# Levels 1 to 4 of a triangular inverse kept as 32 columns per chunk instead of 64

## The chip, the cores and the metric

The kernel runs on one core of one Trainium2 chip. The metric is the device time of one execution in microseconds (us). It was run three times: 2844.94, 2845.5 and 2848.97, median 2845.5. Besides these, one execution was profiled.

## What is computed

A block of two stacked layers on 256 tokens of width 2048. Nearly all of the time goes to its large products with streamed weights. In between stands a recurrent scan (16 heads of 64, two directions, over a context of 256 tokens and then over the 256 tokens of x):

```python
def wkv_scan(r, w, k, v, kk, a, s0, reverse):
    def step(s, inp):
        r_t, w_t, k_t, v_t, kk_t, a_t = inp
        sa = jnp.einsum('bhij,bhj->bhi', s, -kk_t)
        s = (s * w_t[:, :, None, :] + sa[..., None] * (kk_t * a_t)[:, :, None, :]
             + v_t[..., None] * k_t[:, :, None, :])
        return s, jnp.einsum('bhij,bhj->bhi', s, r_t)
    ...
    s_fin, ys = lax.scan(step, s0, xs, reverse=reverse)
```

The kernel computes it in chunks of 64 tokens. Within a chunk the recurrence becomes a linear system, whose 64x64 matrix is triangular with ones on the diagonal, and its inverse is wanted.

## The kernel before

**Units.** The scan is the stretch from about 455 to 880 us of the span. It runs 16 units, `unit(b, q)`: b counts 8 pairs of heads, q is 0 for the context and 1 for x. A unit holds two directions (`d` = 0 and 1), two heads (partitions 0 to 63 and 64 to 127, `HEADS`) and 4 chunks (`NC`) in the free dimension. So a tile of one direction is 128 partitions x 4 x 64 fp32 columns.

**The inverse.** It is built by doubling, levels 0 to 5, with diagonal blocks of 1, 2, 4, ... 32 that become 2, 4, ... 64 wide. POOL masks the matrix for the levels 0 to 4 (`mask_levels`, L990, tiles `lev`, the step named `m0` to `m4`). Level 0 is work of DVE alone: X = I - lev0 (L2058, step X0) and its transpose XT (L2060, step T0). A level `l` from 1 to 4 is then this chain, for each direction:

1. PE, step `Y{l}`: 8 products of lev (the weights, 64x64) with XT (64 moving columns), one for each chunk and head
2. ACT, step `Yb{l}`: copies the result out of PSUM (L1337)
3. PE, step `T{l}`: 8 products of X (the weights) with that copy (64 moving columns)
4. DVE, step `T{l}`: XT = XT - result (L2073)
5. DVE, step `X{l}`: a transpose of XT in blocks of 32x32 gives X (L2043). A level's matrices are zero outside the two diagonal 32x32 blocks, so that this suffices

Y of the next level needs only step 4; step 5 is needed by the PE's T of the next level. Level 5 joins the two 32x32 blocks with 32x32 products (`last_level`, L2690 and L2698, and DVE L2069). XY is a tile with two halves: index 0 holds X, index 1 the copy of step 2.

**Order.** Each engine has its own instruction list, written out by hand, and executes it in order; semaphores (`Steps`, names of steps per direction and q) hold it where it must wait. Both directions alternate in each list. Behind T, PE has other work of the unit as filler (`between`: 12 of 16 records of MV products at levels 1 and 2, a turn of a pair at levels 3 and 4, and in a unit with q = 0 also L2765 and L2743 at level 4). DVE and ACT carry the preparation of the next unit behind each level (`front`, `key`, `group_norm`).

A matmul in fp32 appears as two records in the trace. So one step of both directions, 16 products, shows as 32 records; `each` (L2679) issues them, alternating between the two heads, that is, between two 64x64 quarters of the array.

Of the kernel before, what the change touches and what calls it, by code (L numbers as in the profile page):

```python
# [222 lines left out]
def constants():  # L223
# [24 lines left out]
    for d in range(2):  # L248
# [4 lines left out]
        while size < C:  # L253
# [5 lines left out]
                           np.stack([-(np.arange(P) // SUB % 2 == d).astype(f) for d in range(2)], 1)], 1).astype(f)  # L259
# [22 lines left out]
def program(nc, A, out):  # L282
# [143 lines left out]
    kscan = at("kscan", R + 40 * KIB, [P, 2 * SCAN_DIR + NC * PITCH + C + P + 2])  # L426
# [6 lines left out]
    minus_rows = kscan[:, 2 * SCAN_DIR + NC * PITCH + C + P:]  # L433
# [47 lines left out]
    sub_cols = lambda k: slice(k * SUB, (k + 1) * SUB)  # L481
# [425 lines left out]
    with nc.Block() as block:  # L907
# [162 lines left out]
        def _(act):  # L1070
# [240 lines left out]
            def unit(b, q, ahead=True, norm=None):  # L1311
# [289 lines left out]
        def _(dve):  # L1601
# [429 lines left out]
            def unit(b, q, ahead=True, norm=None):  # L2031
# [438 lines left out]
        def _(pe):  # L2470
# [621 lines left out]
```

How the kernel before makes its waits and increments, by code:

```python
    def wait(self, eng, name, rounds=0):  # L177
        eng.wait_ge(self.sem, self.value(name, rounds))
# [13 lines left out]
    def wait(self, value):  # L192
        self.eng.wait_ge(self.sem, value)
# [607 lines left out]
    def side_step(eng, side):  # L801
        lane, seq, k = side.lane, side.seq, side.k
        tile, c = side_tile(side)
        acc = accs[lane][side.group][:, :]
        if len(tile.shape) == 3:
            acc = acc.rearrange("p (k n) -> p k n", n=CN)
        if seq == 0:
            eng.wait_ge(x_spilled, 16)
            eng.wait_ge(csil_ready, 2)
            eng.wait_ge(mod_used, MOD_CHUNKS)
            eng.wait_ge(mcol_ready, MODS)
        if k == 0 and side.group == 2:
            eng.wait_ge(mcol_ready, MODS + 1)
        eng.wait_ge(raw_in[c.buffer], c.load * 16)
        weight = gain[:, 3, k:k + 1]
        if k == 0:
            ins = eng.tensor_scalar(acc, tile, weight, None, ALU.mult)
        else:
            eng.wait_ge(side_used[lane], seq)
            ins = eng.scalar_tensor_tensor(out=acc, in0=tile, scalar=weight, in1=acc, op0=ALU.mult, op1=ALU.add)
        ins.then_inc(side_used[lane], 1)
# [34 lines left out]
    def load_vectors(eng, which):  # L857
        eng.wait_ge(vec_clear, 1)
        for number, (name, (t, first, n)) in enumerate(VROWS.items()):
            if number % 2 != which:
                continue
# [49 lines left out]
            def load_main(ph, i, j):  # L912
                free = chunks[ph.chunk(i, j)].raw_free
                if free:
                    sp.wait_ge(*free)
                dst, arrives, _ = raw_at(ph, i, j)
```

## Time and profile before

| | |
|---|---|
| median of three runs | 2845.5 us |
| the profiled execution | 2848.24 us, its span 2846.3 us |
| TensorE clock granted, mean | 0.993 of full speed |
| PE busy in the whole span | 97% |
| DVE, ACT, POOL busy | 65%, 47%, 8% |

The span is from the first to the last instruction; the 1.9 us between it and the execution's own time lie around it. Outside the scan the PE is full with wide products. In the scan it is not, and that is where the change works. 0.2% of the time (5.7 us) is about what can be told from no change.

### The profile page before, as it was taken

The numbers are of one execution on the slowest core, as the hardware profiler recorded it, in microseconds if no ns is written. First come the engines' busy times: TensorE is split into PE (matmuls) and PEld (weight loads), VectorE is DVE, ScalarE is ACT, GpSimd is POOL, SyncE is SP. The second block draws the span as 40 slices with busy tenths as digits, with TensorE's granted clock in tenths as the row PEclk, the third lists the DMA queues.
The fourth block names the chain that finished last, engine by engine and source line by source line (L and its number), as shares of the span: only waits on it lengthen the run. The fifth ranks groups of instructions, "written<-read, shape, count | busy, mean of one in ns | idle before, by whom it ended". The sixth has DMA issues, their size and how long they took to land.

```text
span 2846.3 us, 53735 instructions
## 1 busy us (share of the span) xinstructions
PE 2759.5 (97%) x22635; PEld 2312.0 (81%) x22635; DVE 1862.2 (65%) x2553; ACT 1343.2 (47%) x1947; POOL 228.1 (8%) x271
## 2 busy tenths in 40 slices
PE   6999999999989999999999999999999999999998
PEld 2687887878878788888888888888888888888887
DVE  3598787888887766654455656899765545554444
ACT  3222446666664444444444444666544444444443
POOL 1000002323330000000000000233000000000000
PEclk8999999999999999999999999999999999999999
DMA  9998891000004588865665566666566666666564
GB/s 386 363 376 281 258 280 57 8 13 8 8 10 142 168 259 261 260 213 186 191 188 189 188 192 209 193 173 180 174 190 187 192 187 190 190 187 199 190 194 156
DMA packets 470769, 532.14 MB, mean 187 GB/s; under 512 B 22920, under 2 KB 422722, under 8 KB 469634
## 3 DMA queue, kind: packets, MB, share of 16 engines
q1 hardware_dynamic: 464754, 516.13, 56.5%
q0 software_dynamic: 3408, 10.46, 1.1%
q8 instruction: 180, 2.95, 0.4%
q10 hardware_dynamic: 2368, 2.11, 0.3%
q14 instruction: 59, 0.48, 0.0%
HBM read 522.32 MB, written 4.19 MB: 185 GB/s over the span
## 4 chain that ended last, share of the span: by engine, by line
PE 89%; DVE 6%; DMA 2%; issue 1%; ACT 1%; POOL 0%; SPq 0%; ACTq 0%; DVEq 0%
PE ps L2503 14%; PE ps L2514 14%; PE ps L2516 14%; PE ps L2515 14%; PE ps L2504 7%; PE ps L2679 6%; PE ps L3056 4%; PE ps L3057 2%; PE ps L2525 2%; PE ps L2526 2%; PE ps L2527 2%; DMA raw<-in_w_mod 1%; PE ps L2706 1%; PE ps L2575 1%; PE ps L2953 1%
## 5 line engine op out<-in xcount | busy, mean ns | idle before, releaser
L1613 DVE TENSOR_TENSOR lo<-raw,hi 128x1024 fp32r<-128x1024 f32 x776 | 949.0, 1229 | 711.2 <-ACT hi L1085 706.1
L1085 ACT ACTIVATE hi<-raw 128x1024 fp32r<-128x1024 f32 x776 | 820.2, 1059 | 1070.1 <-PE ps L2516 602.9
L2514 PE MATMUL ps<-hi,mov 128*128 128x512 f32 x1408 | 553.8, 393 | 3.6 <-DVE mov L1681 3.6
L2516 PE MATMUL ps<-hi,mov 128*128 128x512 f32 x1408 | 549.6, 390 | 0.0
L2515 PE MATMUL ps<-lo,mov 128*128 128x512 f32 x1408 | 549.2, 390 | 0.0
L2514 PEld LDWEIGHTS ps<-hi,mov 128*128 128x128 f32 x1408 | 265.0, 188 | 58.1 <-issue 4.4
L2516 PEld LDWEIGHTS ps<-hi,mov 128*128 128x128 f32 x1408 | 264.9, 188 | 55.9
L2515 PEld LDWEIGHTS ps<-lo,mov 128*128 128x128 f32 x1408 | 265.2, 188 | 53.8
L2503 PE MATMUL ps<-mov,hi 128*128 128x512 f32 x864 | 306.0, 399 | 0.4 <-DVE mov L2433 0.3
L2503 PE MATMUL ps<-hid,hi 128*128 128x512 f32 x704 | 244.3, 394 | 0.0
L2504 PE MATMUL ps<-mov,lo 128*128 128x256 f32 x864 | 242.6, 281 | 0.0
L2503 PEld LDWEIGHTS ps<-mov,hi 128*128 128x128 f32 x864 | 162.5, 188 | 40.8 <-issue 1.4
L2504 PE MATMUL ps<-hid,lo 128*128 128x256 f32 x704 | 195.3, 277 | 0.0
L3056 PE MATMUL ps<-mov,hi 128*128 128x512 f32 x512 | 185.9, 405 | 0.0
L2504 PEld LDWEIGHTS ps<-mov,lo 128*128 128x128 f32 x864 | 163.2, 189 | 0.1
L2503 PEld LDWEIGHTS ps<-hid,hi 128*128 128x128 f32 x704 | 132.3, 188 | 30.4
L990 POOL TENSOR_TENSOR lev<-U,kscan 128x256 f32<-128x256 f32 x160 | 132.9, 864 | 203.2 <-ACT U L1320 203.2
L3057 PE MATMUL ps<-mov,lo 128*128 128x256 f32 x512 | 143.9, 281 | 0.0
L2504 PEld LDWEIGHTS ps<-hid,lo 128*128 128x128 f32 x704 | 132.2, 188 | 0.0
L2525 PE MATMUL ps<-mov,hi 128*128 128x512 f32 (+1 forms) x288 | 115.0, 399 | 4.8 <-DVE lo L1613 3.6
L3056 PEld LDWEIGHTS ps<-mov,hi 128*128 128x128 f32 x512 | 96.4, 188 | 21.7
L2526 PE MATMUL ps<-mov,hi 128*128 128x512 f32 (+1 forms) x288 | 113.7, 395 | 0.0
(448 smaller groups left out, 4078.4 us busy)
## 6 DMA issues: line engine op xcount, KB each, us to landing
raw<-in_w_in SPq DMA_DIRECT2D x184, 512.0 KB, 4.7
raw<-in_w_gate SPq DMA_DIRECT2D x176, 256.0 KB, 2.9
raw<-in_w_up SPq DMA_DIRECT2D x176, 256.0 KB, 3.2
raw<-in_w_down SPq DMA_DIRECT2D x88, 512.0 KB, 4.6
raw<-in_w_ffn_gate SPq DMA_DIRECT2D x176, 256.0 KB, 2.9
raw<-in_w_ffn_up SPq DMA_DIRECT2D x176, 256.0 KB, 3.1
raw<-in_w_ffn_down SPq DMA_DIRECT2D x88, 512.0 KB, 4.6
raw<-in_w_out SPq DMA_DIRECT2D x64, 512.0 KB, 4.5
```

Source lines behind the costliest of these rows:

```text
L1085: act.activation(hi[:, s, :, :], src, ACT.Copy).then_inc(hi_ready, 1)
L1613: dve.tensor_tensor(lo[:, s, :, :], raw_at(ph, i, j)[0], hi[:, s, :, :].bitcast(F32), ALU.subtract)\
L2503: pe.matmul(ps[:, b, :], hi[:, s, kk, w], moving(k, None), start=first, stop=False)
L2504: mm = pe.matmul(ps[:, b, 0:T], lo[:, s, kk, w], moving(k, 0), start=False, stop=last)
L2514: pe.matmul(out, x(k)[:, 0, tokens], w_hi, start=first, stop=False)
L2515: pe.matmul(out, x(k)[:, 0, tokens], w_lo, start=False, stop=False)
L2516: mm = pe.matmul(out, x(k)[:, 1, tokens], w_hi, start=False, stop=last)
L2525: pe.matmul(ps[0:widths, b, :], hi[:, s, kk, w], mov1[:, k, 0, :, :], start=first, stop=False)
L2526: pe.matmul(ps[0:widths, b, :], hi[:, s, kk, w], mov1[:, k, 1, :, :], start=False, stop=False)
L2679: mm = pe.matmul(ps[hs, 4 * d + bank, off + c * n:off + (c + 1) * n], lhs(c, hs), moving, start=True, stop=True)
L3056: pe.matmul(ps[:, b, :], w_hi[:, kk, :], on_mov(k, None), start=(k == 0), stop=False)
L3057: mm = pe.matmul(ps[:, b, 0:T], w_lo[:, kk, :], on_mov(k, 0), start=False, stop=(k == KB - 1))
```

## The change

Levels 1 to 4 no longer keep the full 64 columns per chunk, half of which are zero. X and XT are each kept as 32 columns per chunk: rows 0 to 31 of a head hold the first diagonal block, rows 32 to 63 the second, in the same 32 columns. Both lie in index 0 of XY (`xc` the first 32 columns, `xtc` the next). The result of Y must be spread again over the block diagonal, as it is now the weights of T: ACT does this with two copies of 32 columns per chunk, each with a scale per partition (`minus_rows`, -1 on one block's rows and 0 on the other's). DVE updates X, and then transposes it to XT. POOL gets a new step `XT` at the end of the levels, which spreads XT over 64 columns for level 5. The diff, without the part that moves `sub_cols` and without the names' slices:

```diff
@@ constants (two more tables of the scan: eye of 32 columns, and the ones of the two diagonal blocks)
-                           np.stack([-(np.arange(P) // SUB % 2 == d).astype(f) for d in range(2)], 1)], 1).astype(f)
+                           np.stack([-(np.arange(P) // SUB % 2 == d).astype(f) for d in range(2)], 1),
+                           np.tile(np.eye(SUB), (P // SUB, 1)), two(np.kron(np.eye(2), np.ones((SUB, SUB))))], 1).astype(f)
@@ names
+    xc, xtc = ([x[:, :, 0, sub_cols(k)] for x in XY] for k in range(2))
+    halves = lambda ap: ap.rearrange("p c (k n) -> p c k n", k=2)
@@ POOL, mask_levels
+                for d in range(2):
+                    scan_dve[d].wait(pool, (q, f"T{LAST - 1}"), b)
+                    scan_pool[d].done(pool.tensor_tensor(halves(XT[q][d]), xtc[d].rearrange("p c (k n) -> p c k n", k=1).broadcast_to([P, NC, 2, SUB]),
+                                                         own_block.rearrange("p (c k n) -> p c k n", c=1, k=2).broadcast_to([P, NC, 2, SUB]), ALU.mult),
+                                      (q, "XT"))
@@ ACT, unit
                         scan_pe[d].wait(act, (q, f"Y{l}"), b)
-                        scan_act[d].done(act.activation(XY[d][:, :, 1, :], in_bank(4 * d + 2, C, 0, C), ACT.Copy), (q, f"Yb{l}"))
+                        for k in range(2):
+                            ins = act.activation(XY[d][:, :, 1, sub_cols(k)], in_bank(4 * d + 2, SUB, 0, SUB), ACT.Copy, scale=minus_rows[:, k:k + 1])
+                        scan_act[d].done(ins, (q, f"Yb{l}"))
@@ DVE, unit
                 def turned(d, l):
-                    own(d, f"T{l}")
-                    done(d, dve.transpose(XY[d][:, :, 0, :], XT[q][d]), f"X{l}")
+                    own(d, f"X{l}")
+                    done(d, dve.transpose(xtc[d], xc[d]), f"T{l}")
...
-                    done(d, dve.tensor_tensor(XY[d][:, :, 0, :], over_chunks(eye64), LEV[0][d][:, :, :], ALU.subtract), "X0")
-                    own(d, "X0")
-                    done(d, dve.transpose(XT[q][d], XY[d][:, :, 0, :]), "T0")
+                    done(d, dve.tensor_tensor(xc[d], over_chunks(eye32), LEV[0][d][:, :, sub_cols(0)], ALU.subtract), "E0")
+                for d in range(2):
+                    own(d, "E0")
+                    done(d, dve.tensor_tensor(xc[d], xc[d], LEV[0][d][:, :, sub_cols(1)], ALU.subtract), "X0")
+                for d in range(2):
+                    turned(d, 0)
...
                         scan_pe[1].wait(dve, (q, f"T{l}"), b)
+                        scan_pool[d].wait(dve, (q, "XT"), b)
...
-                        done(d, dve.tensor_tensor(XT[q][d][:, :, :], XT[q][d][:, :, :], bank(d, 0), ALU.subtract), f"T{l}")
+                        done(d, dve.tensor_tensor(xc[d], xc[d], in_bank(4 * d, SUB, 0, SUB), ALU.add), f"X{l}")
@@ PE, unit
-                        each(scan_pe[d], d, (q, f"Y{l}"), 2, lambda c, hs: LEV[l][d][hs, c, :], lambda c, hs: XT[q][d][hs, c, :])
+                        each(scan_pe[d], d, (q, f"Y{l}"), 2, lambda c, hs: LEV[l][d][hs, c, :], lambda c, hs: xtc[d][hs, c, :], SUB)
...
                         scan_act[d].wait(pe, (q, f"Yb{l}"), b)
-                        scan_dve[d].wait(pe, (q, f"X{l - 1}"), b)
-                        each(scan_pe[d], d, (q, f"T{l}"), 0, lambda c, hs: XY[d][hs, c, 0, :], lambda c, hs: XY[d][hs, c, 1, :])
+                        each(scan_pe[d], d, (q, f"T{l}"), 0, lambda c, hs: XY[d][hs, c, 1, :], lambda c, hs: xc[d][hs, c, :], SUB)
```

On DVE, the piece from level 0 to the first step after level 1, in a unit with q = 1. XY_126 and XY_127 are the tiles XY of the directions 0 and 1, `dirs` here is XT, and scan_pe0 is the semaphore of PE's steps in direction 0. Before:

```order
L2058 TENSOR_TENSOR XY_126<-kscan,lev_128 128x4x64 [waits scan_pe0,scan_pool0]
L2060 STREAM_TRANSPOSE dirs<-XY_126 128x256 [waits scan_dve0]
L2058 TENSOR_TENSOR XY_127<-kscan,lev_129 128x4x64 [waits scan_pe1,scan_pool1]
L2060 STREAM_TRANSPOSE dirs<-XY_127 128x256 [waits scan_dve1]
L1935 SCALAR_TENSOR_TENSOR dirs<-kscan,dirs 128x260 [waits front_act] x2
L2073 TENSOR_TENSOR dirs<-dirs,ps 128x256 [waits scan_pe0]
L2073 TENSOR_TENSOR dirs<-dirs,ps 128x256 [waits scan_pe1]
L2043 STREAM_TRANSPOSE XY_126<-dirs 128x4x64 [waits scan_dve0]
L2043 STREAM_TRANSPOSE XY_127<-dirs 128x4x64 [waits scan_dve1]
L1913 SCALAR_TENSOR_TENSOR knt<-knt,kn 128x512 [waits key_act]
```

and of the change:

```order
L2068 TENSOR_TENSOR XY_126<-kscan,lev_128 128x4x32 [waits scan_pe0,scan_pool0]
L2068 TENSOR_TENSOR XY_127<-kscan,lev_129 128x4x32 [waits scan_pe1,scan_pool1]
L2071 TENSOR_TENSOR XY_126<-XY_126,lev_128 128x4x32 [waits scan_dve0]
L2071 TENSOR_TENSOR XY_127<-XY_127,lev_129 128x4x32 [waits scan_dve1]
L2053 STREAM_TRANSPOSE XY_126<-XY_126 128x4x32 [waits scan_dve0]
L2053 STREAM_TRANSPOSE XY_127<-XY_127 128x4x32 [waits scan_dve1]
L1947 SCALAR_TENSOR_TENSOR dirs<-kscan,dirs 128x260 [waits front_act] x2
L2087 TENSOR_TENSOR XY_126<-XY_126,ps 128x4x32 [waits scan_pe0]
L2087 TENSOR_TENSOR XY_127<-XY_127,ps 128x4x32 [waits scan_pe1]
L2053 STREAM_TRANSPOSE XY_126<-XY_126 128x4x32 [waits scan_dve0]
L2053 STREAM_TRANSPOSE XY_127<-XY_127 128x4x32 [waits scan_dve1]
```

The next level's Y waits for what is in the two rows L2073 before, and for what is in the two rows L2053 of the change: the transposes now stand between the update and the next Y.

On PE, from T of level 1 over Y of level 2 to T of level 2. The first name behind the arrow is the moving operand; where one name stands, it is of both operands. Before:

```order
L2679 MATMUL ps<-tokV,MT_122 64x64 x6
L2679 MATMUL ps<-dirs_141,lev_132 64x64 [waits scan_dve0,scan_pool0]
L2679 MATMUL ps<-dirs_141,lev_132 64x64 x7
L2679 MATMUL ps<-dirs_141,lev_133 64x64 [waits scan_dve1,scan_pool1]
L2679 MATMUL ps<-dirs_141,lev_133 64x64 x7
L2679 MATMUL ps<-tokV,MT_123 64x64 x2
L2679 MATMUL ps<-XY_126 64x64 [waits scan_dve0,scan_act0]
L2679 MATMUL ps<-XY_126 64x64 x7
```

and of the change:

```order
L2693 MATMUL ps<-tokV,MT_122 64x64 x6
L2693 MATMUL ps<-XY_126,lev_132 64x32 [waits scan_dve0,scan_pool0]
L2693 MATMUL ps<-XY_126,lev_132 64x32 x7
L2693 MATMUL ps<-XY_127,lev_133 64x32 [waits scan_dve1,scan_pool1]
L2693 MATMUL ps<-XY_127,lev_133 64x32 x7
L2693 MATMUL ps<-tokV,MT_123 64x64 x2
L2693 MATMUL ps<-XY_126 64x32 [waits scan_act0]
L2693 MATMUL ps<-XY_126 64x32 x7
```

The number of products and their order stay; each moves 32 columns with the same 64x64 weights, and T waits for ACT alone.

On POOL, the end of a unit's masks in the change, with XT (`dirs_141`) new between the masks and the loads of the next pair of heads:

```order
L995 TENSOR_TENSOR lev_136<-U_120,kscan 128x256
L995 TENSOR_TENSOR lev_137<-U_121,kscan 128x256
L999 TENSOR_TENSOR dirs_141<-XY_126,kscan 128x256 [waits scan_dve0]
L999 TENSOR_TENSOR dirs_141<-XY_127,kscan 128x256 [waits scan_dve1]
L983 DMA decw<-in_dec_up 96x2x128 [waits front_pe]
L983 DMA decw<-in_iclr_up 96x2x128
L995 TENSOR_TENSOR lev_128<-U_120,kscan 128x256 [waits scan_act0]
```

Two steps of POOL per unit are added, and each waits for DVE.

## Rows read from the trace of the kernel before

**Rows 1.** The page: busy time, share of the span and instructions of each engine.

```profile
PE 2759.5 (97%) x22635; PEld 2312.0 (81%) x22635; DVE 1862.2 (65%) x2553; ACT 1343.2 (47%) x1947; POOL 228.1 (8%) x271
```

**Rows 2.** Busy time of each engine in a 50 us stretch of the scan.

```profile
core 0: us, PE busy (x) PEld busy (x) DVE busy (x) ACT busy (x) POOL busy (x), PEclk, DMA share, GB/s
600.00:650.00 50.00, 45.75 (x1279) 40.26 (x1275) 42.85 (x103) 33.41 (x82) 18.83 (x23) 1.00 0.04 10
```

**Rows 3.** Timeline, one unit with q = 0, levels 2 to 4 (start, us, engine, ...).

```profile
619.39 1.15 PE L2679 MATMUL ps<-dirs,lev 64*64 64x64 f32 x32 [0.62 <-DVE dirs L2073]
620.11 0.85 ACT L1337 ACTIVATE XY<-ps 128x256 f32<-128x256 f32 x2 [1.09 <-PE ps L2679]
620.54 1.15 PE L2679 MATMUL ps<-XY 64*64 64x64 f32 x32
621.27 0.89 DVE L2073 TENSOR_TENSOR dirs<-dirs,ps 128x256 f32<-128x256 f32 x2 [1.02 <-PE ps L2679]
621.53 0.52 PE L2679 MATMUL ps<-tokV,MT 64*64 64x64 f32 x12
621.88 1.11 PE L2679 MATMUL ps<-dirs,lev 64*64 64x64 f32 x32
...
624.46 1.15 PE L2679 MATMUL ps<-dirs,lev 64*64 64x64 f32 x32
...
626.70 0.44 PE L2725 MATMUL ps<-basics,dirs 128*128 128x128 f32 x2
627.94 0.60 PE L2690 MATMUL ps<-dirs,U 32*32 32x32 f32 x32
```

**Rows 4.** Timeline of PE, one unit with q = 1, levels 2 to 5.

```profile
594.36 1.15 PE L2679 MATMUL ps<-dirs,lev 64*64 64x64 f32 x32
597.13 1.15 PE L2679 MATMUL ps<-dirs,lev 64*64 64x64 f32 x32
...
599.73 1.15 PE L2679 MATMUL ps<-dirs,lev 64*64 64x64 f32 x32
...
602.34 0.66 PE L2690 MATMUL ps<-dirs,U 32*32 32x32 f32 x32
```

**Rows 5.** Timeline of PE: 128-column weights with one moving column, with 128.

```profile
2109.39 1.03 PE L2534 MATMUL ps<-basics,nt 128*128 128x1 f32 x8
...
613.54 0.82 PE L2725 MATMUL ps<-basics,dirs 128*128 128x128 f32 x6
```

**Rows 6.** Lines: duration in ns, least, median and most.

```profile
L2069 DVE SCALAR_TENSOR_TENSOR dirs<-ps,kscan,dirs x32: 340/344/351, 472.8 to 868.5; 128x128 f32<-128x128 f32 x32
L2043 DVE STREAM_TRANSPOSE XY<-dirs x128: 394/417/440, 463.1 to 866.8; 128x256 f32<-128x256 f32 x128
L2073 DVE TENSOR_TENSOR dirs<-dirs,ps x128: 387/420/424, 462.4 to 866.1; 128x256 f32<-128x256 f32 x128
```

**Rows 7.** Timeline of DVE and ACT around the last level of that unit.

```profile
604.17 0.61 DVE L2069 SCALAR_TENSOR_TENSOR dirs<-ps,kscan,dirs 128x128 f32<-128x128 f32 x2 [0.34 <-PE ps L2698]
603.12 0.28 ACT L1334 ACTIVATE XY<-ps 128x128 f32<-128x128 f32 x1 [1.61 <-PE ps L2690]
603.29 0.38 ACT L1343 ACTIVATE tokR<-ps 128x256 f32<-128x256 f32 x1
```

**Rows 8.** Timeline of DVE: the start of level 1 in that unit.

```profile
589.98 0.83 DVE L2058 TENSOR_TENSOR XY<-kscan,lev 128x256 f32<-128x256 f32 x1
591.72 0.45 DVE L2060 STREAM_TRANSPOSE dirs<-XY 128x256 f32<-128x256 f32 x1
592.08 0.74 DVE L1935 TENSOR_TENSOR_SCAN dirs<-kscan,dirs 128x260 f32<-128x260 f32 x1
```

**Rows 9.** The lines of POOL's masks and of two DVE steps, durations.

```profile
L990 POOL TENSOR_TENSOR lev<-U,kscan x160: 712/732/1215, 456.3 to 858.0; 128x256 f32<-128x256 f32 x160
L1913 DVE SCALAR_TENSOR_TENSOR knt<-knt,kn x8: 693/1128/1132, 449.7 to 806.8; 128x512 f32<-128x512 f32 x8
L1915 DVE SCALAR_TENSOR_TENSOR kk<-knt,kk x8: 647/649/684, 451.0 to 812.1; 128x512 f32<-128x512 f32 x8
```

More of the change, by code:

```diff
@@ L425, in program @@
     PITCH = C + 1
-    kscan = at("kscan", R + 40 * KIB, [P, 2 * SCAN_DIR + NC * PITCH + C + P + 2])
+    kscan = at("kscan", R + 40 * KIB, [P, 2 * SCAN_DIR + NC * PITCH + C + P + 2 + SUB + C])
     strict = [kscan[:, d * SCAN_DIR:d * SCAN_DIR + C] for d in range(2)]
@@ L432, in program @@
     less_mean_heads = kscan[:, 2 * SCAN_DIR + NC * PITCH + C:2 * SCAN_DIR + NC * PITCH + C + P]
-    minus_rows = kscan[:, 2 * SCAN_DIR + NC * PITCH + C + P:]
+    minus_rows = kscan[:, 2 * SCAN_DIR + NC * PITCH + C + P:2 * SCAN_DIR + NC * PITCH + C + P + 2]
+    eye32 = kscan[:, 2 * SCAN_DIR + NC * PITCH + C + P + 2:2 * SCAN_DIR + NC * PITCH + C + P + 2 + SUB]
+    own_block = kscan[:, 2 * SCAN_DIR + NC * PITCH + C + P + 2 + SUB:]
     S0 = R + 49 * KIB
@@ L472, in program @@
     stAR = [[x[:, d, 0:2 * NC * C].rearrange("p (k c t) -> p c k t", k=2, c=NC) for d in range(2)] for x in (dirs0, dirs)]
+    sub_cols = lambda k: slice(k * SUB, (k + 1) * SUB)
     XT, AT, BM = stB, U, stK
+    xc, xtc = ([x[:, :, 0, sub_cols(k)] for x in XY] for k in range(2))
+    halves = lambda ap: ap.rearrange("p c (k n) -> p c k n", k=2)
     bcol = lcol[:, 6, 0:4]
@@ L480, in program @@
     sub_rows = lambda h, k: slice((2 * h + k) * SUB, (2 * h + k + 1) * SUB)
-    sub_cols = lambda k: slice(k * SUB, (k + 1) * SUB)
     PLACES = ["head", *FRONT]
@@ L511, in dve_names @@
     def dve_names(q, d):
-        out = (["Q", "R"] if q else []) + ["M", "X0", "T0"]
+        out = (["Q", "R"] if q else []) + ["M", "E0", "X0", "T0"]
         for l in range(1, LEVELS):
-            out += [f"T{l}"] + ([f"X{l}"] if l < LEVELS - 1 else [])
+            out += ([f"X{l}"] if l < LEVELS - 1 else []) + [f"T{l}"]
         out += ["AT"] + (["rho2"] if q else []) + ["Bm"] + (["Y0"] if q else [])
@@ L518, in pool_names @@
     def pool_names(q, d):
-        return [f"m{l}" for l in range(LEVELS - 1)]
+        return [f"m{l}" for l in range(LEVELS - 1)] + ["XT"]
     front_pe, front_act, front_dve = (Steps(sem(k), [(q, n) for q in range(2) for n in names(q)]) for k, names in (
@@ L2038, in unit @@
                 w = C + C * q
-                bank = lambda d, n: in_bank(4 * d + n, C, 0, C)
                 def turned(d, l):
-                    own(d, f"T{l}")
-                    done(d, dve.transpose(XY[d][:, :, 0, :], XT[q][d]), f"X{l}")
+                    own(d, f"X{l}")
+                    done(d, dve.transpose(xtc[d], xc[d]), f"T{l}")
                 for d in range(2 if q else 0):
@@ L2689, in last_level @@
                             of, to = sub_rows(h, 1 - d), sub_rows(h, d)
-                            mm = pe.matmul(ps[to, 2, c * SUB:(c + 1) * SUB], U[d][of, c, sub_cols(d)], XT[q][d][of, c, sub_cols(1 - d)], start=True, stop=True)
+                            mm = pe.matmul(ps[to, 2, c * SUB:(c + 1) * SUB], U[d][of, c, sub_cols(d)], xtc[d][of, c, :], start=True, stop=True)
                     scan_pe[d].done(mm, (q, f"Y{LAST}"))
@@ L2693, in last_level @@
                 for d in range(2):
-                    scan_dve[d].wait(pe, (q, f"X{LAST - 1}"), b)
                     for c in range(NC):
@@ L2697, in last_level @@
                             to = sub_rows(h, d)
-                            mm = pe.matmul(ps[to, 0, c * SUB:(c + 1) * SUB], XY[d][to, c, 0, sub_cols(d)], XY[0][to, c, 1, 0:SUB], start=True, stop=True)
+                            mm = pe.matmul(ps[to, 0, c * SUB:(c + 1) * SUB], xc[d][to, c, :], XY[0][to, c, 1, 0:SUB], start=True, stop=True)
                     scan_pe[d].done(mm, (q, f"T{LAST}"))
```

## The prediction

> **What bounds the kernel now.** I read the page first. PE is busy for 97% of the span and the other engines far less [rows 1], so over the whole kernel PE is the bound. The change touches only the scan, and there the shares are others: in 50 us PE has 45.75 us, DVE 42.85, ACT 33.41 and POOL 18.83 [rows 2]. Nobody is full. What sets the pace must be read from the timeline of one unit.
>
> In the unit with q = 0 [rows 3], Y of level 2 starts at 619.39, T at 620.54, Y of level 3 at 621.88. Y to T is 1.15 us, and the 32 records of Y take 1.15 from first start to last end. ACT starts 0.72 us after the first record of Y, DVE 0.73 after the first of T: that is half of the records (direction 0) and the way through array and PSUM. From 32 records in 1.15 us, with about 0.22 for the last one, a record comes every 0.93/31 = 0.030 us. So 16 records take 0.48, and 0.24 is the way to the consumer. PE thus never waits long: while ACT copies direction 0, PE works on direction 1. The update of DVE takes 0.42 [rows 6] and is covered by direction 1 of T and by the fillers (12 MV records at 621.53). Level 2 takes 2.49 us, level 3 2.58, level 4 3.48, since behind its T stand 1.24 us of fillers (626.70 to 627.94) [rows 3]. In the unit with q = 1, the levels 2 to 4 take 7.98 us together (594.36 to 602.34) [rows 4]. A level is just about balanced between PE's work (2 x 1.08 + 0.4) and the chain of hand-overs.
>
> **The change, part by part.**
>
> *PE's products with 32 moving columns.* This decides. No row shows 64x64 weights with 32 columns, so I bound it. From below: 32x32 weights with 32 columns, L2690, x32 in 0.66 us [rows 4]: with 0.20 for the last, 0.46/31 = 0.015 us per record. From above: 0.030 as now. Which is nearer? Every record has a weight load of its own, and a load that is longer than the moving of columns becomes the pace. The rows with 128-column weights tell this: eight records with ONE moving column take 1.03 us, less 0.25 for the last 0.78/7 = 0.111 us each; six records with 128 moving columns take 0.82, less 0.28 (0.54/5 = 0.108) [rows 5]. One column is no cheaper than 128, so there the load alone sets 0.11 us, 0.87 ns per weight column. For 64 columns that gives 0.055 us per quarter of the array; two quarters alternate, so 0.028 us per record. The 32x32 products fit too: 0.87 x 32 / 2 = 0.014, read 0.015. I take 0.028. The change halves what is moved, but the weights stay 64 wide: 16 records 0.45 us instead of 0.48, almost nothing.
>
> The Trainium skill, TensorE: Matmul & The Clock Gate, section LDWEIGHTS (loading the stationary operand), says that a load takes the weights' column count over 1.2 in ns, whatever the contraction; that is 53 ns for 64 columns, or 0.027 per record as an estimate, and the rows above agree.
>
> *ACT.* One copy of 256 columns becomes two of 128. One of 128 takes 0.28 us, and the next instruction starts 0.17 after it [rows 7]. So the pair is done 0.45 after its start, where the single copy of 256 took 0.38 (0.85 for both directions, the second waiting for PE) [rows 3].
>
> *DVE.* An update of 256 columns takes 0.42, a transpose 0.42 [rows 6]. From PSUM 128 columns take 0.34 in L2069, a costlier operation [rows 6], and its second starts 0.61 - 0.36 = 0.25 after the first [rows 7]. Without the cost of 128 columns (0.13 at the slope of about 1 ns per column, an estimate) 0.42 becomes 0.28; bounds 0.24 and 0.34. I take 0.28 for both, and 0.22 until the next may start. But the order changes: XT, which the next Y wants, is now made by the transpose, and in DVE's list the transpose of direction 0 stands behind the update of direction 1, which waits for T of direction 1.
>
> *The chain of a level, from Y of direction 0 at 0.* Y0 to ACT: 0.45 + 0.24 = 0.69; its pair of copies ends at 1.14. Y1 is there at 1.14, its copies end at 1.59. T0 starts at 1.19, T1 at 1.64 (0.05 for a semaphore). Update 0 is at 1.88, update 1 at 1.64 + 0.69 = 2.33; transpose 0 starts at 2.55, ends at 2.83; next Y0 at **2.88**. PE's fillers (0.4) fit into the gap after T1's last record at 2.09 and hide nothing more. The transposes used to hide behind Y; now that cover is gone.
>
> *Sum.* q = 0: levels 2 and 3, 2 x 2.88 - 5.07 = +0.69. Level 4: T1 issued at 2.09, then the 1.24 of fillers: 3.33 against 3.48, -0.15. q = 1: 3 x 2.88 - 7.98 = +0.66.
> Level 1, q = 1: DVE needs 2.10 us for four steps before the scans (589.98 to 592.08 [rows 8]); six of half width come to about 1.8, so the scans behind them end 0.3 earlier, but Y of level 1 for direction 0 starts some 0.25 later behind both directions' steps, and then the same long chain runs: +0.1. For q = 0 masks and scans set it: 0.
> POOL's XT: two steps of 0.73 each, at most 1.2 [rows 9], from the start of level 5 on. Their reader L2069 comes 1.83 us behind it (602.34 to 604.17) [rows 4, 7], direction 1 about 2.1: 1.5 fits, with 0.5 to spare. But while POOL works, DVE is slower: 1.13 at L1913 beside the masks against 0.65 at L1915 without [rows 9]. With q = 0, two such steps of preparation stand before L2069; +0.1.
> The larger table's load is 6% more of one DMA before the scan: 0.
> Eight of each: 8 x (0.69 - 0.15 + 0.66 + 0.1 + 0.1) = **+11 us**. The profiled execution took 2848.24 (span 2846.3), 2.7 above the median of 2845.5; the sum is a difference and goes on the median: 2856.5 us.
>
> **The rivals.**
>
> *The moving columns do set PE's pace* (faster). Then a record takes 0.015: 16 take 0.24. Chain: Y0 to ACT 0.48, copies end 0.93 and 1.27; T0 0.98, T1 1.32; update 1 at 1.80, transpose ends 2.30, next Y at 2.35. q = 0: 4.70 - 5.07 = -0.37, level 4 at 1.56 + 1.24 = 2.80, -0.68; q = 1: 7.05 - 7.98 = -0.93. Sum -16 us: 2830. For it: the 32x32 rows [rows 4]. Against it: the single-column rows [rows 5]. The price at which it turns: at 0.022 the same chain gives 2.58 a level, and the sum is q = 0 +0.09 and -0.45, q = 1 -0.24: -5 us. So about 0.024 per record is break-even. 15%.
>
> A fixed floor of start to start would lie between. The row that shows 0.015 speaks against one above that [rows 4]; at 0.025 the chain gives 2.73, sum +4 us. The Trainium skill, same page, section "Wait — 56ns, not 53.3ns?", names about 25 ns as such a floor however few columns; by the row just named it doesn't hold for small products on several parts of the array. Within the next case.
>
> *The chain is shorter than I lay it out* (no change). If DVE's hand-overs take 0.2 less in a level (0.24 per operation, next start after 0.17, no 0.05 on top), a level takes 2.68: 8 x (0.29 - 0.15 + 0.06 + 0.1 + 0.1) = +3 us: 2848.5. For it: DVE has less to do, 8 x 0.2 us per unit. 20%.
>
> *POOL's XT comes late* (slower still). If contention stretches both steps to 1.2, they end 2.4 behind the start of level 5, 0.3 after they are wanted. 16 x 0.3 = 5 more: 2861. 10%; the forecast itself 55%.
>
> **How the numbers follow.** Forecast 2856.5, its own range 2852 to 2861. 8 in 10 takes in the no-change case and the late POOL, and part of the faster one: 2840 to 2865. Chances, with 0.2% = 5.7 us, which is about what a measurement tells from no change: slower is the forecast and late POOL, 0.65; faster 0.14, the rest 0.21.
>
> **What the changed profile would show.** The 64x64 products with 32 columns as 32 records in about 1.1 us, not 0.66; the levels 2 and 3 at 2.8 to 2.9 us from Y to Y; PE waiting before Y for the transpose (DVE XY) and before T for ACT; DVE and ACT not busier. DVE's busy time in the scan falls by some 36 us (256 steps x 0.14) and nobody gains. I am wrong if the 32 records take 0.7 us, or if PE's wait before Y is not there.

## The result, and the profile after

The changed kernel takes 2993.06 us (four runs, 2991.43 to 2997.03) against 2847.16 for the kernel before in the same comparison (2844.94 to 2848.97): ratio 1.0516, interval 1.0503 to 1.0529. It is slower by 146 us; +11 was forecast, and the range ended at 2865.

The page of the changed kernel, its busy line and the row of the granted clock in 40 slices of 74.7 us:

```profile
PE 2879.0 (96%) x22635; PEld 2422.8 (81%) x22635; DVE 1853.1 (62%) x2585; ACT 1373.5 (46%) x2075; POOL 254.2 (9%) x303
PEclk9999997767776899999999999999999999999999
```

PE's busy time went **up** by 120 us (before: [rows 1]), though it has less to do. The second row says where: from the seventh slice to the fourteenth, which is the scan, TensorE was granted 0.6 to 0.8 of full speed. So the first view must be that of the windows. The same one for the whole scan, in the kernel before and, below it, in the one after (length, busy time with number of instructions of PE, weight loads, DVE, ACT and POOL, granted clock, DMA share, GB/s):

```profile
455.00:876.00 421.00, 382.68 (x10538) 336.03 (x10540) 349.90 (x833) 277.04 (x684) 146.99 (x181) 0.99 0.03 9
```

```profile
455.00:1020.00 565.00, 506.29 (x10512) 450.72 (x10512) 338.88 (x860) 307.76 (x812) 172.56 (x213) 0.72 0.02 7
```

The scan is longer by 144 us, nearly the whole difference, and its mean clock falls from 0.99 to 0.72. Windows of 2 us in the unit after (q = 0) show how:

```profile
666.00:668.00 2.00, 2.00 (x15) 1.84 (x13) 1.64 (x3) 1.47 (x5) 2.00 (x4) 1.00 0.00 0
668.00:670.00 2.00, 0.58 (x6) 0.21 (x5) 2.00 (x6) 1.03 (x3) 2.00 (x3) 1.00 0.00 0
670.00:672.00 2.00, 1.90 (x57) 1.76 (x58) 1.90 (x4) 1.38 (x6) 2.00 (x4) 0.98 0.02 4
672.00:674.00 2.00, 1.99 (x38) 1.83 (x37) 1.38 (x5) 1.10 (x3) 1.70 (x2) 0.50 0.00 0
680.00:682.00 2.00, 2.00 (x34) 1.92 (x34) 0.48 (x2) 1.98 (x7) 0.00 (x0) 0.50 0.04 8
686.00:688.00 2.00, 2.00 (x10) 1.51 (x8) 1.79 (x5) 0.20 (x1) 1.20 (x2) 0.50 0.00 0
688.00:690.00 2.00, 1.56 (x61) 1.03 (x61) 0.53 (x1) 0.68 (x3) 1.03 (x1) 0.76 0.00 0
690.00:692.00 2.00, 2.00 (x38) 1.58 (x28) 1.70 (x5) 0.93 (x4) 0.21 (x1) 1.00 0.03 8
```

PE waits for most of 668 to 670 and works on narrow products after that. From 672 on the clock is at 0.50, which is the level of 1.2 GHz. It stays there for 17 us although PE is now busy for 1.92 to 2.00 of every 2.00 us, and returns after the wide products at the end of the levels. The PE's timeline of the same unit (start, time, line, tile, shape, records; in brackets the idle time before and what ended it):

```profile
669.93 1.12 PE L2693 MATMUL ps<-XY,lev 64*64 64x32 f32 x32 [1.42 <-DVE XY L2053]
670.85 0.34 PE L2693 MATMUL ps<-tokV,MT 64*64 64x64 f32 x4
671.30 1.53 PE L2693 MATMUL ps<-XY 64*64 64x32 f32 x32
672.64 0.88 PE L2693 MATMUL ps<-tokV,MT 64*64 64x64 f32 x12
673.53 1.92 PE L2693 MATMUL ps<-XY,lev 64*64 64x32 f32 x32
678.06 1.92 PE L2693 MATMUL ps<-XY,lev 64*64 64x32 f32 x32
682.47 1.92 PE L2693 MATMUL ps<-XY,lev 64*64 64x32 f32 x32
686.58 1.06 PE L2778 MATMUL ps<-gsq,basics 128*128 128x256 f32 x2
688.42 0.80 PE L2704 MATMUL ps<-XY,U 32*32 32x32 f32 x32
```

The same step, Y with 32 records, takes 1.12 us at full clock and 1.92 at half. Level 2 takes 4.53 us (673.53 to 678.06) against 2.49 [rows 3], and PE no longer waits in it: at half clock it is itself the pace. Of the 64 Y steps of the scan 51 run at half clock (mean granted clock under 0.6) and one in part; in the kernel before none does, and one in part (at 854.50, mean clock 0.68).

### The profile page after: what moved, and what is told of

It is laid out like the page before. It is cut to its first block, busy times and chain, and to the rows that moved or that the text cites. A ratio compares the mean times of both kernels' runs of the same rounds, so it can differ in the third digit from the quotient of the medians.

```text
span 2989.8 us, 53808 instructions
## 1 busy us (share of the span) xinstructions
PE 2879.0 (96%) x22635; PEld 2422.8 (81%) x22635; DVE 1853.1 (62%) x2585; ACT 1373.5 (46%) x2075; POOL 254.2 (9%) x303
## 4 chain that ended last, share of the span: by engine, by line
PE 88%; DVE 7%; DMA 2%; issue 2%; ACT 1%; SPq 0%; ACTq 0%; POOL 0%; DVEq 0%
PE ps L2517 14%; PE ps L2528 13%; PE ps L2530 13%; PE ps L2529 13%; PE ps L2693 9%; PE ps L2518 7%; PE ps L3068 3%; PE ps L2539 2%; PE ps L2540 2%; PE ps L3069 2%; PE ps L2541 2%; PE ps L2738 1%; PE ps L2719 1%; DMA raw<-in_w_mod 1%; PE ps L2589 1%
## 5 line engine op out<-in xcount | busy, mean ns | idle before, releaser
L2517 PEld LDWEIGHTS ps<-mov,hi 128*128 128x128 f32 x864 | 162.2, 188 | 41.0 <-issue 1.4
L2693 PEld LDWEIGHTS ps<-XY,lev 64*64 64x64 f32 x2048 | 106.0, 203 | 52.9 <-issue 35.1
L2693 PE MATMUL ps<-XY,lev 64*64 64x32 f32 x2048 | 112.5, 277 | 36.6 <-DVE XY L2053 35.3
L995 POOL TENSOR_TENSOR lev<-U,kscan 128x256 f32<-128x256 f32 x160 | 126.6, 825 | 160.1 <-ACT U L1330 160.1
L1348 ACT ACTIVATE XY<-ps,kscan 128x128 f32<-128x128 f32 x256 | 78.7, 364 | 116.7 <-PE ps L2693 116.5
```

What stands on the lines that cost most here:

```text
L1348: ins = act.activation(XY[d][:, :, 1, sub_cols(k)], in_bank(4 * d + 2, SUB, 0, SUB), ACT.Copy, scale=minus_rows[:, k:k + 1])
L2517: pe.matmul(ps[:, b, :], hi[:, s, kk, w], moving(k, None), start=first, stop=False)
L2693: mm = pe.matmul(ps[hs, 4 * d + bank, off + c * n:off + (c + 1) * n], lhs(c, hs), moving, start=True, stop=True)
```

## The experiments

All of the first group build on the changed kernel, but for the second of them, and were timed beside the kernel before (2846.57 us).

**e1_move64**: the changed kernel, but both products move the 64 columns of `xc` and `xtc`; one half of each result is not used. All waits, orders and steps stay.

```diff
-  each(..., f"Y{l}"), 2, ..., lambda c, hs: xtc[d][hs, c, :], SUB)
+  each(..., f"Y{l}"), 2, ..., lambda c, hs: XY[d][hs, c, 0, :])
-  each(..., f"T{l}"), 0, ..., lambda c, hs: xc[d][hs, c, :], SUB)
+  each(..., f"T{l}"), 0, ..., lambda c, hs: XY[d][hs, c, 0, :])
```

> The changed kernel, but both products of the levels 1 to 4 move 64 columns again (X and its transpose together; each consumer reads the 32 it needs). Order, waits, weights and the work of DVE, ACT and POOL stay those of the change. Theory A (the clock of TensorE falls because each record moves only 32 columns): granted clock in the scan back at 0.97 to 1.00, 2870 to 2885 us; what is left above 2847 is the longer chain and level 0. Theory B (the clock falls because PE waits in every level for DVE and ACT): clock stays near 0.73 in the scan, 2950 us or more.

Measured: 2912.22 us (2910.11 to 2913.05), ratio 1.0228 (1.0213 to 1.0243). Moving twice as many columns makes the changed kernel 81 us **faster**. Its scan window:

```profile
455.00:940.00 485.00, 401.47 (x10501) 348.61 (x10494) 339.57 (x862) 302.61 (x811) 172.52 (x213) 0.96 0.03 8
```

The clock is back at 0.96, a little below the 0.97 of theory A; the time is 27 us above the range of that theory. A unit with q = 1 in which it fell for a while and came back, by PE's timeline:

```profile
611.86 1.97 PE L2693 MATMUL ps<-XY,lev 64*64 64x64 f32 x32 [2.62 <-DVE XY L2053]
616.44 1.81 PE L2693 MATMUL ps<-XY,lev 64*64 64x64 f32 x32
620.35 1.15 PE L2693 MATMUL ps<-XY,lev 64*64 64x64 f32 x32 [0.35 <-DVE XY L2053]
621.75 1.20 PE L2693 MATMUL ps<-XY 64*64 64x64 f32 x32 [0.25 <-ACT XY L1348]
623.65 1.15 PE L2693 MATMUL ps<-XY,lev 64*64 64x64 f32 x32 [0.34 <-DVE XY L2053]
626.86 0.63 PE L2704 MATMUL ps<-XY,U 32*32 32x32 f32 x32 [0.24 <-DVE XY L2053]
```

Two things are read here. At full clock 32 records take 1.15 us with 64 columns and 1.12 with 32: halving the columns gives 0.03 us, next to nothing, as forecast. And behind a wait of 2.62 us products of 64 columns can also start at half clock, but they get the full clock back within the unit, which those of 32 don't. The wait alone doesn't decide it. Six units with q = 1 wait 2.55 to 2.67 us before level 1, in both kernels. With 32 columns all six begin it at half clock; with 64 two do, one does in part, and three keep the full clock.

**e2_before_move32**: the kernel before, in which both products move only 32 columns and the readers take them twice. Half of the result of a level is left out.

```diff
-  each(..., f"Y{l}"), 2, ..., lambda c, hs: XT[q][d][hs, c, :])
+  each(..., f"Y{l}"), 2, ..., lambda c, hs: XT[q][d][hs, c, 0:SUB], move=SUB)
-  each(..., f"T{l}"), 0, ..., lambda c, hs: XY[d][hs, c, 1, :])
+  each(..., f"T{l}"), 0, ..., lambda c, hs: XY[d][hs, c, 1, 0:SUB], move=SUB)
```

> The kernel before, but both products of the levels 1 to 4 move only 32 of the 64 columns, and their readers take those 32 twice; half of the result of a level is left out. Order and waits are those of before. Theory A (few columns per record): clock falls to 0.7 to 0.85 in the scan and the time rises to 2920 to 2980 us although nothing waits longer. Theory B (waits): clock stays at 0.97 to 1.00, 2840 to 2850 us.

Measured: 2904.57 us (2893.87 to 2919.33), ratio 1.0206 (1.0171 to 1.0241). With the order and the waits of before, the narrow products alone cost 58 us (47 to 73 by the single executions). Theory A had 2920 or more and a clock of 0.85 at most, theory B 2850 at most; the result lies between, nearer to A. The profiled execution took 2893.87 and is the fastest of the four, so that the clock of the others was lower than in its scan window:

```profile
455.00:921.00 466.00, 428.16 (x10495) 381.30 (x10494) 350.76 (x833) 276.47 (x682) 145.76 (x181) 0.86 0.03 8
```

**e3_y64**: only Y moves 64 columns, T moves 32 (the first pair of lines of e1).

> The changed kernel with only Y moving 64 columns, T moving 32. Theory A: clock in the scan between that of the change (0.73) and 1.00, 2880 to 2960 us. Theory B: as the change, 2985 to 3000 us, or longer by the columns of Y.

Measured: 2926.55 us (2914.16 to 2932.61), ratio 1.0274 (1.0245 to 1.0303), clock in the scan 0.90. It lies between, nearer to e1: one of two products narrow costs 14 of the 81 us (2 to 20 by the single executions).

**e4_tiles32**: the changed kernel with 16 products of 32x32 weights for each step in place of 8 of 64x64, and one copy on ACT, since nothing has to be spread.

```diff
-  each(..., f"Y{l}"), 2, lambda c, hs: LEV[l][d][hs, c, :], ...)
+  for c in range(NC):
+      for h in range(2):
+          for k in range(2):
+              to = sub_rows(h, k)
+              mm = pe.matmul(ps[to, 4 * d + 2, ...], LEV[l][d][to, c, sub_cols(k)], xtc[d][to, c, :], ...)
```

> The changed kernel with the weights cut too: both products as 16 products of 32x32 weights and 32 columns per direction instead of 8 of 64x64, so that ACT needs one copy of 128 columns instead of two. If the weights' width sets the pace, a direction's 32 records take 0.25 to 0.5 us at full clock (0.0075 to 0.015 each). Theory A: the clock stays low (0.6 to 0.8) as no record moves more, time 2930 to 3010 us. Theory B (waits): the clock stays low as well. If the fall came from the pace of weight loads instead, the clock recovers and the time is 2860 to 2880 us.

Measured: 2993.6 us (2991.84 to 2995.42), ratio 1.0516 (1.0499 to 1.0534): the same as the changed kernel. PE's timeline at full clock:

```profile
601.70 0.83 PE L2700 MATMUL ps<-XY,lev 32*32 32x32 f32 x64 [1.42 <-DVE XY L2051]
602.72 0.75 PE L2700 MATMUL ps<-XY 32*32 32x32 f32 x64
```

64 records take 0.83 us where 32 wider ones took 1.12, so the products did become quick. Its scan window, and the waits of its PE there (engine and line, what was waited for: us in total, times, longest):

```profile
455.00:1020.00 565.00, 446.05 (x14567) 374.47 (x14568) 339.03 (x858) 266.00 (x688) 173.04 (x213) 0.71 0.03 8
PE ps L2700 <- issue: 51.9, 51, 2.2
```

The clock is as low as in the changed kernel (0.71 and 0.72). PE is busy for 60 us less (446.05 against 506.29), but in place of that it stands idle on "issue", that is, without a wait that the profile shows: 51.9 us at these products, where the changed kernel has none. What holds PE there is open, so the equal times are a coincidence. e4 shows that narrower weights don't bring the clock back, and not what they would be worth.

The second group takes the other 66 us (e1 against before) apart, beside a kernel before of 2848.7. All but f4 build on e1.

**f1_skip_half_level0**: one of the two subtractions per direction in level 0 left out.

```diff
-  done(d, dve.tensor_tensor(xc[d], over_chunks(eye32), LEV[0][d][:, :, sub_cols(0)], ALU.subtract), "E0")
-  ...
-  done(d, dve.tensor_tensor(xc[d], xc[d], LEV[0][d][:, :, sub_cols(1)], ALU.subtract), "X0")
+  done(d, dve.tensor_tensor(xc[d], over_chunks(eye32), LEV[0][d][:, :, sub_cols(0)], ALU.subtract), "X0")
```

> As e1_move64 (the changed kernel with 64 columns moved, 2912 us), but level 0 on DVE has one subtraction of 128 columns per direction instead of two: the second diagonal block's level 0 is left out. In the trace of the change such a subtraction takes 0.81 us beside POOL's masks, both operands from SBUF. Theory: it stands on the path to Y of level 1, so two of them cost 1.6 us in each of 16 units: 2884 to 2892 us. If it only delays what waits anyway: 2905 us or more.

Measured: 2884.9 us (2883.28 to 2889.82), ratio 1.0129 (1.0114 to 1.0144): 27 us less than e1, clock 0.99. DVE's groups by line in the scan of the changed kernel, from 455 to 900 us (records, busy time, mean ns of one | idle time before them), say why:

```profile
L2053 DVE STREAM_TRANSPOSE XY<-XY 128x128 f32<-128x128 f32 x128 | 31.7, 285 | 0.0
L2087 DVE TENSOR_TENSOR XY<-XY,ps 128x128 f32<-128x128 f32 x103 | 29.2, 286 | 120.0 <-PE ps L2693 119.9
L2071 DVE TENSOR_TENSOR XY<-XY,lev 128x128 f32<-128x128 f32 x26 | 20.0, 808 | 0.0
L2068 DVE TENSOR_TENSOR XY<-kscan,lev 128x128 f32<-128x128 f32 x26 | 18.4, 747 | 4.2 <-PE ps L2738 2.4 <-POOL lev L995 1.5
```

128 columns with one operand from PSUM (L2087) take 286 ns; the same with both operands in SBUF, while POOL masks (L2071), take 808.

**g3_pool_after_x0** (third group, before at 2847.6) shows that this is POOL. It builds on e1; POOL starts the masks of level 1 only when DVE is done with level 0's subtractions.

```diff
+                        if l == 1:
+                            scan_dve[1].wait(pool, (q, "X0"), b)
```

> As e1_move64 (2912 us), but POOL starts its masks of level 1 only when DVE's level 0 is done. The result is the same. If DVE's subtractions take 0.81 us because POOL works beside them: the last three or four of them take about 0.29 us in the trace, Y of level 1 starts about 1 us earlier, 2893 to 2900 us. If 0.81 us is the cost of their shape: they stay at 0.81 us, and the time rises by the wait of POOL, 2920 us or more.

Measured: 2890.51 us (2887.64 to 2892.33), ratio 1.0152 (1.0135 to 1.0168), 22 us less than e1. The same two groups (both lines are two further down), the second now with POOL idle beside it; the first still meets a mask of level 0 in some units (277 to 800 ns):

```profile
L2070 DVE TENSOR_TENSOR XY<-kscan,lev 128x128 f32<-128x128 f32 x32 | 11.0, 382 | 4.6 <-PE ps L2740 2.8 <-POOL lev L997 1.5
L2073 DVE TENSOR_TENSOR XY<-XY,lev 128x128 f32<-128x128 f32 x32 | 7.7, 280 | 0.0
```

808 became 280. The Trainium skill, SBUF — State Buffer, section "Who interferes with whom", says that a DVE instruction with two SBUF inputs contends with a GpSimd instruction that reads SBUF, since its second input comes through the read interface that they share. The trace agrees: 808 ns beside GpSimd (POOL), 280 without.

**f2_turn_at_once**: DVE turns a direction right behind its update, in place of both updates first.

```diff
                         done(d, dve.tensor_tensor(xc[d], xc[d], in_bank(4 * d, C, 0, SUB), ALU.add), f"X{l}")
-                    for d in range(2 if l < LEVELS - 1 else 0):
                         turned(d, l)
```

> As e1_move64 (2912 us), but DVE turns direction 0 right behind its update instead of behind the update of direction 1. The result is the same. Theory: the order on DVE costs about 0.48 us a level (update 1 starts 0.52 behind update 0 and the transpose stands behind it), so 64 levels give 25 to 30 us: 2882 to 2890 us. If ACT's longer copies hold T and Y alone: 2900 us or more.

Measured: 2893.13 us (2890.39 to 2897.4), ratio 1.0157 (1.0142 to 1.0172): 19 us less than e1. Rows of its timeline:

```profile
638.53 1.20 PE L2692 MATMUL ps<-XY,lev 64*64 64x64 f32 x32
639.25 1.15 ACT L1348 ACTIVATE XY<-ps,kscan 128x128 f32<-128x128 f32 x4
641.07 0.44 PE L2737 MATMUL ps<-basics,dirs 128*128 128x128 f32 x2
641.44 0.37 PE L2692 MATMUL ps<-XY,lev 64*64 64x64 f32 x5
```

The last row is cut off by the end of the view. A level falls from 3.30 to 2.91 us (638.53 to 641.44), and PE goes from the filler straight on to the next Y. The time is 3 us above the range expected.

**f3_one_copy**: one ACT copy of 256 columns with a constant scale in place of two of 128 with a scale per partition. The zeros outside the blocks are left out.

```diff
-  for k in range(2):
-      ins = act.activation(XY[d][:, :, 1, sub_cols(k)], in_bank(...), ACT.Copy, scale=minus_rows[:, k:k + 1])
+  ins = act.activation(halves(XY[d][:, :, 1, :]), ..., ACT.Copy, scale=-1.0)
```

> As e1_move64 (2912 us), but ACT spreads Y with one copy of 256 columns per direction with a constant scale instead of two of 128 with a scale per partition; the zeros outside of the diagonal blocks are left out, so the inverse is another one. A pair takes 0.62 us in the trace of e1_move64, one copy of 256 took 0.38 before. Theory: 0.25 to 0.3 us a level, 64 levels: 2892 to 2897 us. If DVE's order holds the level: 2905 us or more.

Measured: 2894.52 us (2893.37 to 2896.99), ratio 1.0161 (1.0146 to 1.0177): 18 us less than e1. In the changed kernel's page one such copy takes 364 ns:

```profile
L1348 ACT ACTIVATE XY<-ps,kscan 128x128 f32<-128x128 f32 x256 | 78.7, 364 | 116.7 <-PE ps L2693 116.5
```

**f4_fill**: the changed kernel (32 columns) with two products of 128x128 weights and 256 columns, which nobody reads, between Y and T of each level from 1 to 4. It asks whether more work on PE brings the clock back.

```diff
                     between(b, q, l, ahead, range(0, l not in (3, LAST)))
+                    for _ in range(2 if l < LAST else 0):
+                        pe.matmul(ps[:, 4, T:2 * T], ident, basics[:, 0:2, :], start=True, stop=True)
```

> The changed kernel (32 columns moved, 2993 us) with two extra products of 128x128 weights and 256 columns between Y and T in each of the levels 1 to 4; their result is read by nobody. They use PE while it waits for ACT. Theory A (the clock falls because PE has too little to move in the time): clock in the scan up from 0.72 to 0.9 or more, and the time falls to 2910 to 2950 us although there is more work. If the clock doesn't care for such products, the time rises by their 0.43 us in 64 levels: 3010 to 3050 us.

Measured: 3058.95 us (3051.85 to 3060.2), ratio 1.0739 (1.0721 to 1.0757). That is above both ranges expected. Rows of PE's timeline, a unit with q = 0 and then one with q = 1:

```profile
614.42 1.12 PE L2693 MATMUL ps<-XY,lev 64*64 64x32 f32 x32 [1.41 <-DVE XY L2053]
615.62 1.13 PE L2850 MATMUL ps<-basics 128*128 128x256 f32 x4
626.52 1.12 PE L2693 MATMUL ps<-XY,lev 64*64 64x32 f32 x32 [0.34 <-DVE XY L2053]
...
648.58 1.92 PE L2693 MATMUL ps<-XY,lev 64*64 64x32 f32 x32 [2.66 <-DVE XY L2053]
650.70 2.07 PE L2850 MATMUL ps<-basics 128*128 128x256 f32 x4
668.55 1.92 PE L2693 MATMUL ps<-XY,lev 64*64 64x32 f32 x32
```

Half a success. Where the clock was full it now stays full to level 4 (31 Y steps of 64 at half clock, not 51; mean clock 0.79). Where it was already low, behind the longer wait of a unit with q = 1, the wide products run at half clock as well (2.07 us) and don't raise it. What they cost outweighs it: a level takes 4.08 us in place of 3.24 at full clock, and 6.75 in place of 4.53 at half clock. That extra work of this kind restores the clock, wherever it is put, has fallen.

The third group, beside g3, asks how the narrow products and the waits act together.

**g1_move32_half_level0**: the changed kernel with f1's edit (half of level 0 left out).

> The changed kernel (32 columns, 2993 us) with one subtraction of level 0 per direction left out. In the change PE waits 2.6 us before Y of level 1, and the clock is at its lower level from level 1 on until the wide products behind level 5. If that wait brings the fall about: clock in the scan 0.95 or more, 2885 to 2900 us. If the narrow columns keep it low by themselves: the clock stays at 0.70 to 0.80 and only the 27 us of f1_skip_half_level0 go: 2960 to 2975 us.

Measured: 2959.07 us (2946.63 to 2964.02), ratio 1.0387 (1.0359 to 1.0415), clock 0.74. Rows of its PE timeline, and its windows around them:

```profile
626.13 1.12 PE L2690 MATMUL ps<-XY,lev 64*64 64x32 f32 x32 [1.21 <-DVE XY L2053]
627.50 1.92 PE L2690 MATMUL ps<-XY 64*64 64x32 f32 x32
630.12 1.92 PE L2690 MATMUL ps<-XY,lev 64*64 64x32 f32 x32
```

```profile
624.00:626.00 2.00, 0.91 (x5) 0.46 (x3) 1.97 (x5) 1.28 (x3) 2.00 (x4) 1.00 0.00 0
626.00:628.00 2.00, 1.87 (x46) 1.72 (x48) 1.97 (x3) 1.18 (x5) 2.00 (x3) 0.79 0.03 8
628.00:630.00 2.00, 2.00 (x40) 1.92 (x37) 0.82 (x4) 1.30 (x3) 2.00 (x4) 0.50 0.00 0
```

In a unit with q = 1 the wait before level 1 is down from 2.66 us (as in f4's row) to 1.21, and Y of level 1 runs at full clock; the clock falls a step later instead. Level 0's wait is thus not the one cause of the fall: in the units with q = 0 PE doesn't wait before level 1 at all, and the clock falls in level 3 or 4 in six of the eight. 64 columns are worth 74 us here (f1 against g1).

**g2_all_three**: e1 with the edits of f1, f2 and f3 together, and what they leave out.

> e1_move64 (2912 us) with the edits of f1 (27 us), f2 (19) and f3 (18) together; part of level 0 and the zeros outside of the blocks are left out. If these three terms are the whole difference to the kernel before and add up: 2845 to 2853 us. If they cover each other: 2855 to 2870 us.

Measured: 2853.47 us (nine runs, 2849.91 to 2857.71), ratio 1.0023 (1.0013 to 1.0032). The three take back 59 of e1's 66 us; one by one they gave 27, 19 and 18, together 64. 6 us are left over to its kernel before (2847.6), the remainder of the 66. Its scan window is nearly that of before:

```profile
455.00:882.00 427.00, 387.80 (x10539) 341.20 (x10540) 322.88 (x832) 278.55 (x684) 169.81 (x213) 0.99 0.03 9
```

**g4_all_three_move32**: the same with 32 columns moved.

> As g2_all_three, but with 32 columns moved as in the change. The waits of PE are as short as they get here, so this shows the columns alone. Theory: the clock still falls in part of the units, as in e2_before_move32 (2905 us, 0.87 in the scan): 2890 to 2920 us. If long waits are needed for the fall: clock 0.97 or more and 2835 to 2850 us, as fast as before or faster.

Measured: 2883.44 us (2880.59 to 2886.82), ratio 1.0128 (1.0113 to 1.0144), clock 0.89. With the waits short again the narrow products cost 30 us. That is 7 us below the range of the theory that the clock still falls in part of the units, and far above that of the other (2850 at most); the clock falls in 4 of the 16 units for three levels or more.

| waits | 64 columns moved | 32 moved | difference | clock with 64, with 32 |
|---|---|---|---|---|
| those of before (before, e2) | 2846.57 | 2904.57 | 58 | 0.99, 0.86 |
| f1, f2, f3 taken out (g2, g4) | 2853.47 | 2883.44 | 30 | 0.99, 0.89 |
| half of level 0 out (f1, g1) | 2884.9 | 2959.07 | 74 | 0.99, 0.74 |
| those of the change (e1, after) | 2912.22 | 2993.06 | 81 | 0.96, 0.72 |

The kernel before was timed anew for each group, at 2846.57 to 2848.7, so that a difference across groups is sure to some 2 us. The price of the narrow products doesn't simply follow the waits. Before level 1 of most units with q = 1 PE waits 0.87 us in the first row, 1.21 in the second and third, and some 2.6 in the last. Over the scan, PE with 64 columns is idle for 38, 39, 65 and 84 us (length less busy time). So the two rows with much waiting have the high prices, but with 38 and 39 us of it the prices are 58 and 30. What makes them differ is open.

No version beat the kernel before; g2, the nearest, leaves work out.

## Why the prediction was wrong

The sign was right and the reason given for it was a real part, but the step that failed is one that the prediction does not even name: it took every duration from rows at full clock and let the granted clock stand through the change. [rows 2] shows 1.00, and the text never asked what holds it there. In its place the runs show a clock of 0.72 in the scan in place of 0.99, and 81 us that go when 64 columns are moved again (e1). Nor was the rest well sized: with the 64 columns the change still costs 66 us, six times the 11 forecast. Point by point:

**PE's products with 32 columns.** Right. 0.028 us per record was taken; 32 records take 1.12 us at full clock (after) and 1.15 with twice the columns (e1). The rival by which the moving columns set the pace is refuted. But "almost nothing" was wrong as a cost: the halved columns cost 81 us through the clock (after against e1), 58 in the unchanged order (e2). In the two profiled executions, 79.6 us apart (2991.76 and 2912.15), the levels 1 to 4 of the 16 units, from the first Y to the first product of level 5, take 282.2 us in the changed kernel and 221.6 in e1, 61 more. The 15 stretches from there to the next unit's first Y take 266.7 and 249.5, 17 more. So nearly all of it is found in the scan, three quarters of it in the levels.

**The chain of a level.** Mechanism right, size off. Forecast 2.88 us, at full clock 3.30 (e1, 620.35 to 623.65). Two terms make up most of it. ACT's pair was taken as 0.45 us from copies without a scale per partition [rows 7]; it takes 0.62, one copy 364 ns against 277; the pairs of both directions, one behind the other, take 1.14 in place of 0.90, which is 0.24 of the 0.42. The Trainium skill, ScalarE: Activation LUTs, section "What ACT_TABLE_LOAD costs", states that each per-partition operand adds about 93 ns. The trace agrees with 87; an estimate by it, 277 + 93 = 370 ns for one copy, would have been right. Another 0.10 is hand-overs on DVE: the next Y starts 0.65 us after update 1 does (623.00 to 623.65), forecast 0.55. The last 0.08 is in smaller hand-overs. For these levels +9.6 us was forecast (8 x (0.69 - 0.15 + 0.66)). In e1, at full clock, it is 29: with q = 0 the levels 2 and 3 take 6.60, that is +1.53, and level 4 3.76 in place of 3.48, +0.28; with q = 1 3.30 + 3.30 + 3.21 = 9.81 in place of 7.98, +1.83; times 8. f2 and f3 took out 19 and 18, together more than 29: they shorten level 1 as well, which is not in this sum (in a unit with q = 1 from 3.30 to 2.91 us by f2). That the transpose loses its cover behind the other direction was foreseen, and f2 confirms it.

**Level 0.** Wrong, 27 us (f1) where +0.8 was put. Of the 27 some 5 are clock: e1 still has five Y steps at half clock and f1 none, and its levels 1 to 4 take 216.5 us in place of 221.6. The stretches between, with level 0 in them, take 226.5 in place of 249.5; before they took 223.5. "Six of half width come to about 1.8" scaled the time with the columns. Two of each three steps read both operands from SBUF beside POOL's masks, and take 0.75 to 0.81 us each, however narrow. The row for this was already there: L2058 takes 0.83 us [rows 8], twice the 0.42 of an update of the same 256 columns with one operand in PSUM [rows 6]. It was half of the story: L2058 of the other direction, behind a transpose, takes 0.46 in every unit, though POOL works there too, and one of POOL's masks beside it 0.90 in place of 0.72. So a place beside POOL doesn't fix the price by itself; the four subtractions in a row of the change took 0.70 to 0.81 each. The prediction knew of the contention, from [rows 9], and put it on POOL's XT alone, where it matters little.

**POOL's XT.** Two steps of 1.02 us mean, above the 0.73 assumed and below the rival's 1.2. In e1 its reader waits for it three times, 1.0 us in all, where the rival had 5; the late-XT rival is out.

**The faster rival's sums.** -16 and -5 us leave out the two terms of 0.1 that the forecast has; with them they are -14 and -3. It changes nothing, as the rival is refuted by its first term.

**The signs named for the changed profile.** 32 records in 1.1 us and PE's wait before Y for the transpose came, the latter where the clock was full. The levels at 2.8 to 2.9 us did not (3.24 at full clock, 4.53 at half), ACT was busier (307.76 us against 277.04 in the scan), and DVE's busy time fell by 11 us (349.90 to 338.88) where 36 was named: level 0 took most of the saving. None of the signs looked at the clock.

The whole of +146 us: 81 by the clock, 27 by level 0 (5 of it clock again), 19 by DVE's order, 18 by ACT's copies. That only 1 us is left is luck: g2 finds the last three 5 us less when taken out together, and no part is surer than some 2 us.

## What to carry to other kernels

A stretch in which PE is busy through many small products can depend on its clock more than on their work, as here: when a change makes them smaller or puts waits between them, ask first whether the full clock will hold, and look at the granted clock of the windows before anything else in the result. Padding a product with useless columns can be the faster choice. And an operand moved from PSUM to SBUF, or a DVE step split in two, is priced by a row of its own kind beside POOL's work, not by its width.

## What the runs showed of the hardware

- With 32 moving columns, PE busy for 2.00 of 2.00 us in the trace stayed at 0.50 of its clock to the end of a unit's levels; with 64 columns, at the same count of records, it came back (e1: 1.97, 1.81, 1.15 us for the same step). So PE's busy time in the trace doesn't tell its clock. The Trainium skill, TensorE: Matmul & The Clock Gate, section "What's actually happening", says that the throttled state is the default and that activity releases it. The trace agrees in the two levels, 0.50 and 1.00. What decides between them these runs leave open.
- The clock is not a matter of columns alone: the price of 32 was 30 and 58 us with short waits and 74 and 81 with long ones (table above), and the long waits alone, with 64 columns, brought the clock down only to 0.96. Behind the same wait of 2.6 us products of 64 columns ran at full clock in some units and at half in others.
- Wide products put in between kept a full clock (31 steps of 64 at half clock in place of 51) but did not raise a low one in the same unit.
- Narrower weights are quick at full clock: 64 records of 32x32 weights in 0.83 us, 0.010 each after the last one's 0.2. But in e4 PE also stood idle for 51.9 us at them without a wait that the profile shows.
- A DVE subtraction of 128x128 with both operands in SBUF took 808 ns beside POOL's masks and 280 without (g3).
